# Eight fixed experts in two quads, a rebuilt final normalisation, and expert weight buffers of eight feature rows of one matrix

## The reference

```python
h = layer_norm(ALPHA * x + merged @ w_out, ln1_g, ln1_b)
# MoE: 32 experts in 4 groups of 8; each token takes its best group, and in it the best two experts
hid = silu(tok @ w_g[e]) * (tok @ w_u[e]) * combine[:, e]      # 2048 -> 256
moe = sum over e of hid_e @ w_d[e]                              # 256 -> 2048
ple = sigmoid(h @ w_pg) * (p @ w_pp)
y   = layer_norm(ALPHA * h + moe + ple, ln2_g, ln2_b)
```

## Time and profile before

| | us |
|---|---|
| median of 3 runs (1585.72, 1590.06, 1596.23) | 1590.06 |
| the profiled execution | 1587.91 |
| its span from the first to the last instruction | 1586.0 |
| PE busy, share of the span | 1421.7, 90% |
| DVE busy, share of the span | 763.3, 48% |
| gate and up loads | 128 + 128 DMAs of 512 KB |
| down loads; PLE gate loads | 64; 16 DMAs of 1024 KB |

### The profile page before, as it was taken

One profiled execution on the slowest core, in us unless ns is written; L12 is line 12 of the kernel. 1 busy time (PEld: TensorE's weight loads), 2 busy tenths in 40 slices (PEclk: granted clock), 3 DMA queues, 4 the chain that ended last, 5 costly groups with the idle time before them and its releaser, 6 DMA issues.

```text
span 1586.0 us, 21185 instructions
## 1 busy us (share of the span) xinstructions
PE 1421.7 (90%) x8709; PEld 1079.3 (68%) x8709; DVE 763.3 (48%) x1506; ACT 341.4 (22%) x480; POOL 95.8 (6%) x96
## 2 busy tenths in 40 slices
PE   6969999999999999998999997966989899799971
PEld 4968998777778678767999996522747474356320
DVE  3749877888874336314567446311121303220437
ACT  3423232000010010003334334231211121111102
POOL 3730000000010100000010000100000000000002
PEclk9979999999999789978999997888999999899986
DMA  8425444333333432333565464799999999999991
GB/s 219 155 82 160 158 146 147 107 106 107 106 115 115 137 108 99 119 126 94 181 194 180 157 235 147 301 391 407 385 340 403 408 389 348 409 389 404 409 371 56
DMA packets 139103, 353.25 MB, mean 223 GB/s; under 512 B 20676, under 2 KB 21788, under 8 KB 138480
## 3 DMA queue, kind: packets, MB, share of 16 engines
q1 hardware_dynamic: 135944, 341.99, 59.8%
q0 software_dynamic: 3056, 9.83, 2.1%
HBM read 344.61 MB, written 7.18 MB: 222 GB/s over the span
## 4 chain that ended last, share of the span: by engine, by line
PE 79%; DMA 9%; DVE 7%; issue 2%; ACT 1%; SPq 1%; DVEq 0%; ACTq 0%
PE bank L518 77%; DMA mslot<-in_w_exp_up 5%; DMA mslot<-in_w_exp_down 3%; DVE atok L2396 1%; SPq L1183 1%; DVE lo L1604 1%; PE bank L533 1%; ACT hi L1330 1%; DMA stS<-in_state_hgrn 1%; DMA ident<-in_consts 1%; DVE stS L1926 0%; DVE stats L2480 0%; DVE outl L2404 0%; DVE nmr L2492 0%; DVE ws L1773 0%
## 5 line engine op out<-in xcount | busy, mean ns | idle before, releaser
L518 PE MATMUL bank<-XT,raw 128*128 128x264 f32 x1280 | 309.3, 402 | 0.0
L518 PEld LDWEIGHTS bank<-XT,raw 128*128 128x128 f32 x1280 | 250.5, 198 | 47.3 <-issue 3.2
L1604 DVE TENSOR_TENSOR lo<-raw,hi 128x2048 fp32r<-128x2048 f32 x68 | 159.0, 2339 | 133.9 <-ACT hi L1330 133.9
L1330 ACT ACTIVATE hi<-raw 128x2048 fp32r<-128x2048 f32 x68 | 130.2, 1914 | 236.0 <-PE bank L518 232.9
L518 PE MATMUL bank<-mslot,Xg 128*32 128x512 f32 (+1 forms) x1024 | 147.1, 664 | 31.0 <-DMA mslot<-in_w_exp_up 29.8
L518 PE MATMUL bank<-XH,hi 128*128 128x264 f32 x512 | 148.9, 291 | 7.4 <-DVE lo L1604 6.2
L518 PE MATMUL bank<-XL,hi 128*128 128x264 f32 x512 | 147.2, 287 | 0.0
L518 PE MATMUL bank<-XH,lo 128*128 128x264 f32 x512 | 146.2, 286 | 0.0
L518 PEld LDWEIGHTS bank<-mslot,Xg 128*32 128x32 f32 (+1 forms) x1024 | 39.7, 124 | 115.2 <-issue 114.4
L518 PE MATMUL bank<-HT,mslot 128*128 128x264 f32 x512 | 116.5, 387 | 0.0
L518 PEld LDWEIGHTS bank<-HT,mslot 128*128 128x128 f32 x512 | 96.5, 190 | 18.0 <-issue 1.7
(11 more groups left out here) (409 smaller groups left out, 2245.0 us busy)
## 6 DMA issues: line engine op xcount, KB each, us to landing
raw<-in_w_in SPq DMA_DIRECT2D x72, 1024.0 KB, 5.1
mslot<-in_w_exp_gate SPq DMA_DIRECT2D x128, 512.0 KB, 10.1
mslot<-in_w_exp_up SPq DMA_DIRECT2D x128, 512.0 KB, 12.1
mslot<-in_w_exp_down SPq DMA_DIRECT2D x64, 1024.0 KB, 14.9
raw<-in_w_out SPq DMA_DIRECT2D x16, 1024.0 KB, 5.0
mslot<-in_w_ple_gate SPq DMA_DIRECT2D x16, 1024.0 KB, 15.0
raw<-in_w_branch_b SPq DMA_DIRECT2D x8, 1024.0 KB, 5.0
raw<-in_w_branch_a SPq DMA_DIRECT2D x8, 1024.0 KB, 5.1
```

Of the source, the lines that this page charges most:

```text
L518: return nc.tensor.matmul(out, w, x, start=start, stop=stop)
L1330: nc.scalar.activation(hi[:, s % RH, :], raw[:, n % RD, :], ACT.Copy).then_inc(hi_done, 1)
L1604: v.tensor_tensor(lo[:, n % RD, :], raw[:, n % RD, :], hi[:, s % RH, :].bitcast(F32), ALU.subtract).then_inc(lo_done, 1)
```

## The change

1. **Plan.** `FIXED = 8`, `WIDE = 12`: groups 0 and 1 are experts 0 to 7; the pairs hold places 8 to 11 and stay groups 4 and 5. Blocks are now [0,1], [2,3], [4,5], [6,7], [8]; PLE groups 2, 3, 6, 7 instead of 2, 3, 4, 7. The first gather serves two groups (256 columns) and stands before s = 0 and s = 1.
2. **Buffers.** A chunk holds eight feature rows of gate or of up alone: one DMA of 1 MB in runs of 8 KB; a quarter is then 32 matmuls of 256 columns. s = 0 is gate and s = 1 up over features 0 to 7 (of 16), s = 2 and 3 the same over 8 to 15.
3. **Gathers** in `between` move from s = 0 to 3 (two each) to s = 1 (two), 2 (two), 3 (four).
4. **The end.** Group 8's down chunks come in three pieces (columns 0:1024, 1024:1536, 1536:2048), with the scatter of a piece behind the matmuls of the next. Gain and bias are loaded as 8 rows of 512 (`ln2row`), issued behind group 7's down loads; PE spreads them to 128 partitions with 8 matmuls (`norm_rows`) behind s = 3 of group 8, ACT copies them. Statistics are taken column block by column block as the adds finish; the norm itself is two `scalar_tensor_tensor` per half row on DVE, from `atok` into `ynorm`, stored in halves; the flag is read after it.
5. **Router.** The seven small DVE steps that pick a token's expert logits become one product and one reduction.

```diff
-FIXED = 4
-WIDE = 8
+FIXED = 8
+WIDE = 12
...
-PLANS = [[list(range(FIXED))] + QUADS[:4] + PAIRS[2:4] + QUADS[4:]] + [PAIRS] * 4
-BLOCKS = [[[0], [1, 2], [3, 4], [5, 6], [7, 8]]] + ...
-PLE_AT = {2: 0, 3: 1, 4: 2, 7: 3}
+PLANS = [[[0, 1, 2, 3], [4, 5, 6, 7]] + QUADS[:2] + PAIRS[4:6] + QUADS[2:]] + [PAIRS] * 4
+BLOCKS = [[[0, 1], [2, 3], [4, 5], [6, 7], [8]]] + ...
+PLE_AT = {2: 0, 3: 1, 6: 2, 7: 3}
-FIRST_GATHER = {0: (0, 1, 2), 1: (3, 4), 2: (5, 6, 7), 3: ()}
+FIRST_GATHER = {0: (0, 1, 2, 3), 1: (4, 5, 6, 7), 2: (), 3: ()}
...
+            return ((0, 2), (2, 3), (3, 4)) if (rnd, g) == (0, len(PLANS[0]) - 1) else ((0, 2), (2, 4))
...
-                    for k in range(4):
-                        kx = 4 * s + k
+                    out = slice(FE * (s % 2), FE * (s % 2 + 1))
+                    for k in range(8):
+                        kx = 8 * (s // 2) + k
                         for i in range(ne):
...
-                            last = mm(bank[4][rows, :].rearrange("p (i f) -> p i f", i=2),
-                                      Xg[:, kx, x:x + width], w[:, k], kx == 0, kx == 15)
+                            last = mm(bank[4][rows, out], Xg[:, kx, x:x + width],
+                                      mslot[slot[i] % RM][:, k * FE:(k + 1) * FE], s == 0 and k == 0, s == 3 and k == 7)
...
+                        if nxt is not None and s:
+                            for u in ((), (0, 1), (2, 3), (4, 5, 6, 7))[s]:
+                                gather(rnd, nxt, u)
...
+                        if (rnd, g, s) == (0, groups - 1, 3):
+                            norm_rows(0)
...
-                down(rnd, groups - 1)
-                for nb in range(4):
-                    scatter(rnd, groups - 1, nb)
+                down(rnd, groups - 1, lambda nb: scatter(rnd, groups - 1, nb))
+
+            def norm_rows(again):
+                pe.wait_ge(ln2_ld, 32)
+                for r in range(8):
+                    b = side(("row", again, r))
+                    mm(b[:, :], ident[0:8, r:r + 1].to_broadcast([8, 128]), ln2row[:, :], True, True).then_inc(
+                        misc_ready, 1)
...
+                        src = t[("w_exp_gate", "w_exp_up")[s % 2]][0, expert(g, i)].rearrange(
+                            "o (p k) f -> p (o k) f", p=P)
+                        k0 = 8 * (s // 2)
+                        sp.dma_start(mslot[c % RM].rearrange("p (k f) -> p k f", k=8),
+                                     src[:, k0:k0 + 8, :]).then_inc(m_land[c % RM], 16)
...
                     if g:
                         down_load(g - 1)
+                    if rnd == 0 and g == len(plan) - 1:
+                        sp.wait_ge(misc_ready, misc["ple", 3, 2][0] + 1)
+                        for i, n in enumerate(("ln2_gain", "ln2_bias")):
+                            sp.dma_start(ln2row[4 * i:4 * i + 4, :], t[n][0].rearrange("(r n) -> r n", r=4)).then_inc(
+                                ln2_ld, 16)
                 down_load(len(plan) - 1)
-                gate_up_done(sp, rnd, len(plan) - 1)
-                for i, n in enumerate(("ln2_gain", "ln2_bias")):
-                    sp.dma_start(ln2[:, i, :], t[n].to_broadcast([P, D])).then_inc(ln2_ld, 16)
...
+                for tt, (t0, tn) in enumerate(TOK):
+                    for step in range(2):
+                        for half in range(2):
+                            cs = slice(1024 * half, 1024 * (half + 1))
+                            if step == 0:
+                                v.scalar_tensor_tensor(out=ynorm[0:tn, tt, cs], in0=atok[0:tn, tt, cs],
+                                                       scalar=mv[0:tn, tt, 0:1], in1=ln2[0:tn, 0, cs],
+                                                       op0=ALU.subtract, op1=ALU.mult).then_inc(gained, 1)
+                            else:
+                                dve.wait_ge(gained, 6 * again + 2 * tt + half + 1)
+                                v.scalar_tensor_tensor(out=ynorm[0:tn, tt, cs], in0=ynorm[0:tn, tt, cs],
+                                                       scalar=rstd[0:tn, tt:tt + 1], in1=ln2[0:tn, 1, cs],
+                                                       op0=ALU.mult, op1=ALU.add).then_inc(f_out, 1)
```

More of the change, by code:

```diff
@@ L1011, in down @@
                 stored(("hid", rnd, g))
-                for h in range(2):
+                for h, (n0, n1) in enumerate(pieces(rnd, g)):
+                    if after is not None and h:
+                        for nb in range(*pieces(rnd, g)[h - 1]):
+                            after(nb)
                     slot = [m_at["d", rnd, g, h, i] for i in range(ne)]
@@ L1015, in down @@
                         m_landed(pe, slot[i])
-                    for q in range(2):
-                        nb = 2 * h + q
+                    for nb in range(n0, n1):
                         banks_free(nb)
@@ L1088, in _ @@
                     expert_round(rnd)
+                norm_rows(1)
         @block.sync
@@ L1556, in expert_round @@
                     silu(rnd, g)
+                    if (rnd, g) == (0, groups - 1):
+                        norm_rows(0)
                     for u in range(early, 8 if nxt is not None else early):
@@ L1563, in expert_round, with norm_rows, final_norm @@
                 store(rnd, groups - 1)
+            def norm_rows(again):
+                for r in range(8):
+                    b, read = side(("row", again, r))
+                    if r == 0:
+                        gate_up_done(act, *((4, len(PLANS[4]) - 1) if again else (0, len(PLANS[0]) - 1)))
+                    nc.scalar.activation(ln2[:, r // 4, (r % 4) * 512:(r % 4 + 1) * 512], b[:, :],
+                                         ACT.Copy).then_inc(read, 1)
+            def final_norm(again):
+                act.wait_ge(f_var, again + 1)
+                nc.scalar.activation(rstd[:, :], rstd[:, :], ACT.Sqrt).then_inc(f_sq, 1)
             expert_round(0)
+            nc.scalar.activation(warm[:, :], ones[:, 0:1], ACT.Sqrt)
+            final_norm(0)
             act.wait_ge(flag_ready, 1)
@@ L2457, in expert_round, with final_link, row_statistics @@
                 give_back(rnd, groups - 2)
-                give_back(rnd, groups - 1)
+                if rnd == 0:
+                    last_give_back(groups - 1)
+                else:
+                    give_back(rnd, groups - 1)
+            tail = sem("final_chain")
+            done = [0]
+            def final_link(ins):
+                done[0] += 1
+                ins.then_inc(tail, 1)
+            def row_statistics(nb):
+                for tt, (t0, tn) in enumerate(TOK):
+                    final_link(v.bn_stats(stats[0:tn, tt, nb, :], atok[0:tn, tt, nb * 512:(nb + 1) * 512]))
```

200 lines of the change are left out of this document (93 added, 107 removed).

## The result

The changed kernel takes 1612.11 us (median of 4 runs, 1610.78 to 1612.28) against 1591.12 of the kernel before: a ratio of 1.0124, 95% interval 1.010 to 1.0148 (the ratios given here go over all runs of both kernels and are not quite the quotient of the medians). It is about 21 us slower; the forecast was 1587.2 with a range of 1570 to 1602. The profiled execution is 1612.28 with a span of 1610.4.

A forecast was written before the change was run, and what follows sets the result against it. The expert stage was taken as bound by loads and PE in turn, plus its two ends. Runs -3, narrow matmuls 0, start 0, `ln2row` wait +17, tail -14.7 sum to -0.7: 1587.2 us from 1587.9, no change, interval 1570 to 1602.

The forecast's parts named there:

- the start: First gather and quarter of the expert stage: first quarter done 1.4 us later, net 0, between -3 and +11.
- Rival D: First gather: it stays at 1.2 GHz throughout, +10 us, 1597; chance 0.13.
- The wait for `ln2row`: Behind group 8's last quarter: PE waits 13 us for the gain's load, holding up `down` 7; +17 us.
- Rival B: End of the stage: the wait for `ln2row` is short, +7 instead of +17, 1577; chance 0.17.
- The 8 KB runs: Gate/up loads: 8 KB packets take 314 ns against 328 for two of 4 KB; -3 us, between 0 and -13.
- rival E: Gate/up loads: 8 KB runs are cut into 4 KB packets, gain 0, 1590; chance 0.07.
- Rival A: Gate/up loads: the short runs pay nearly in full, -13 instead of -3, 1577; chance 0.15.
- Matmuls of 256 columns: Gate/up quarters: weight loads hide under 0.22 us matmuls, a quarter stays about 3.5 us plus a tail; 0.
- rival C: Every `gate_up` pass: weight loads bind the narrow matmuls, at least +60 us, 1647; 1603 at 0.27 us passes; chance 0.08.
- The tail: From the last `down` matmul to the end: 26.7 us against 41.4, -14.7, by 3 either way.
- signs of being wrong: Quarters over 4.4 us; no idle PE gap before the `ln2row` matmuls; group 8's quarter 3 ending ten or more us from 1503.

The follow-up runs named there:

- warm: The changed kernel with 34 idle matmuls in PE's waits between the last dense block and the first gather; 1601.92 us.
- narrow: The changed kernel with a first gather of group 0 alone (128 columns), group 1 gathered later as its own block; 1591.46 us.
- wide_small: The changed kernel with the first gather's 8-row sample matmuls made over 128 rows of other tokens, for times alone; one run took 1589.3 us.
- halves: early_narrow with the `down` of group 8 in two halves again and its four scatters behind both; 1583.38 us.
- early_row: The changed kernel with the gain and bias rows loaded before group 3 into a place of their own; 1594.0 us.
- rows128: early_row with the eight gain and bias rows in a zero-filled tile of 128 rows, so the spread's matmuls go over 128 rows; 1590.13 us.
- early_narrow_zero: early_narrow with the first gather's 8-row matmuls made over 128 rows, rows 8 to 127 zero, no idle matmuls; 1569.52 us.
- early_narrow_warm: early_narrow with 19 idle matmuls in PE's waits before the first gather; 1574.13 us.
- early_narrow_gaps: early_narrow with the eight matmuls that spread gain and bias moved behind the pieces of the last `down`; 1573.41 us.
- early_narrow: The changed kernel with the edits of early_row and narrow together; 1577.23 us.

## Why the prediction was wrong

**The step that failed is the start.** It stood at 0 and measured +16.0 at the first quarter. The prediction wrote: "I assume the doubled gather, which streams without pause, raises it after some 4 us: 9 at 0.44 and 39 at 0.22, 13 us." With all passes over 128 rows that is what happens, nearly to the number: 12.57 us, the first quarter at D + 34.8, 1.1 behind the kernel before where 1.4 was forecast. The gather of this kernel isn't made of such passes. A third of them go over 8 rows, and it ran 25.3 us at 1.2 GHz. The row to read was there: in the earlier trace rows the old gather stays at the lower clock for 11 us, and the clock rises once the dense quarter runs. I saw it and took "longer" for the cure. The price was there too: 36 matmuls of 128 columns at half of my 0.44 us would have been 7.9 us, and they took 11.2, the 8-row passes and the changes to them included. Rival D named the low clock, with 0.13, and gave it 10 us; it had neither the changes between 128 and 8 rows (25.3 instead of 48 x 0.44 = 21.1) nor the slow quarter that follows (5.91 instead of 3.66). That the loss is carried through to the end, the runs warm, narrow and wide_small show: each keeps at t what it gains at the first quarter or more (warm 8.7 and 9.4, narrow 10.5 and 16.2, wide_small 14.9 and 19.2).

**The wait for `ln2row`: mechanism right, size off.** Forecast: a stall of 13 us, landing at t + 14.5, +17 in all. Measured: 12.51, the spread from t + 14.0, +25.3. The mis-sized terms are the ones at a low clock: `norm_rows` 14.02 for the 10 that I chose between 7 and 14, `down` 7 9.56 for 7.2, and 26.7 instead of 24.2 from there to E. The early load takes 17.7 us out of E - t; 7.6 are left (46.4 against 38.8). Of these the scatters between the pieces, for which the prediction had 4, are 2.6: halves moves them behind E and comes to 43.8, and since it loses 7.4 in all they are worth their place. The other 5.0 stay in halves: there the second half of `down` 8 begins at t + 38.5, behind its wait of 4.10 us for chunks, and takes 5.34; in the kernel before it began at t + 35.2, waited for no chunk, and took 3.64. What makes these chunks later no run separates. Rival B, a short wait, is out.

**The 8 KB runs: mechanism right, too small.** -3 was forecast, 4.3 (at the end) to 6.5 (from the first quarter to t) measured, inside its bounds of 0 and -13; packets of 314 ns were right, so rival E is out. One reading made it small: the 220 us in which loads set the pace leave out 1407 to 1472, where the earlier trace rows has a DMA share of 1.03 too. Rival A, -13 in full, is not what happened, but the stage from the first quarter to t gained more than I gave the runs, 2 to 3 us of it unexplained.

**Matmuls of 256 columns: right.** A quarter is 3.66 us where 3.64 stood; rival C, the only one on the slower side by more than 1%, is out.

**The tail: right.** -13.6 for -14.7, 27.8 for 26.7; a half row of `scalar_tensor_tensor` took 1.2 where I had 1.15.

The sum, from D: +16.0 - 8.7 + 25.3 - 13.6 = +19.0, where -0.7 was forecast: 16.0 from the start, 8.3 from the end, 1.1 from the tail, less 5.7 that the stage gained beyond the -3. Of the signs of being wrong that the prediction named, two came: quarter 3 of group 8 ended at 1518.45 and not near 1503 (5.3 of these 15 us lie ahead of D), and some quarters took over 4.4 us, the first 5.91, at a low clock and not for want of weight loads (3.66 at 1035.88).

## What to carry to other kernels

Matmuls over 8 rows cost more here than their columns: put such a matmul where PE's clock doesn't matter, or fill its operand with rows of zeros, and read the granted clock over an operation of the same make before you assume that a longer one will raise it. A small load issued behind large ones can land when they do (here 16 KB, some 12 us behind their issue), so load it as soon as its place is free; a wait for it in PE's queue is paid by everything behind. When an edit takes 10 us off an engine and the kernel gains nothing, look at what that engine waits for next: here it was the chunks of `down` 7.

## What the runs showed of the hardware that I had not expected

- PE can be busy without a pause and still have a granted clock of 0.50: 25.2 of 25.5 us in the first gather, 14.0 us in the spread. Between streams of 128-row passes at 1.00 a spread of 8-row matmuls even let the clock fall (early_row, at 1522.5, PE busy before and after). The same counts of passes over 128 rows hold it (rows128) or raise it (wide_small, early_narrow_zero), also where 120 of the rows are zero. The Trainium skill's page "TensorE: Matmul & The Clock Gate", section "What's actually happening", has the clock follow how busy PE is; in this case busy by the trace was not enough, and the rows in use decided. In the gather the few rows and the changes between 128 and 8 go together; in the spread there are no such changes, so there the rows alone did it.
- A gather with its 8-row matmuls raised a low clock in no run (25.3 us at 0.50). A high one it held in some places and not in others: it ran 13.45 us at 1.00 in warm and 13.55 in the second gather of the changed kernel, but in the kernel before the clock fell in the gathers that begin at 1005.26 (1.00 up to 1006.8, 0.50 from 1007 to 1015.2), and in early_narrow_warm it fell right behind them. What separates these cases no run shows.
- Each step from 128 rows to 8 and back costs 0.38 us at 2.4 GHz (1.68 against 1.30). It is the change that costs: 16 passes over 8 rows one behind the other took 14.02 us at 0.50, twice the 7.10 of 16 passes over 128 rows at 1.00. The Trainium skill's page "TensorEngine Tiling (Array Packing)", section "Key Properties", says that a change of tiling mode drains the engine; the 0.38 us would fit that if passes over 8 rows go in another mode than passes over 128, which no run here shows.
- The same code up to D ended between 961.3 and 969.0 in 14 profiles, so that two kernels can seem to differ by several us for that reason: the profiled executions of early_narrow_gaps and early_narrow are 3.1 us apart (1573.41 and 1576.55), their D 3.6, and from D the one that seems faster is 0.6 longer.
